# A third set of expert weight buffers and a six-expert TensorE loop in a mixture-of-experts decoder layer

## The reference

```python
def hier_moe(h, rg_w, rg_b, re_w, re_b, w_gate, w_up, w_down):
    ...                         # top-1 of 4 groups, top-2 of the 8 experts inside it
    for e in range(N_EXPERTS):  # 32
        y = (jax.nn.silu(t @ w_gate[e]) * (t @ w_up[e])) @ w_down[e]
        out = out + combine[:, e:e + 1] * y
```

## Time and profile before

| | us |
|---|---|
| three runs | 1025.98, 1027.39, 1028.46 |
| span of the profiled execution (first to last instruction) | 1026.5 |
| TensorE busy (matmuls) | 866.4 |
| first expert begins on TensorE | 460.98 |
| last matmul of expert 31 ends | 996.0 |

### The profile page before, as it was taken

The page is one execution under the profiler, slowest core; times in us unless marked ns, Lnnn a source line. Parts: engine busy times, 40 slices in busy tenths (PEclk is TensorE's granted clock), DMA queues, the critical chain, the costliest instruction groups (busy, mean ns, idle before and its releaser), DMA issues.

```text
span 1026.5 us, 15037 instructions
## 1 busy us (share of the span) xinstructions
PE 866.4 (84%) x5337; PEld 581.7 (57%) x5338; DVE 324.9 (32%) x576; ACT 194.9 (19%) x286; POOL 224.5 (22%) x270
## 2 busy tenths in 40 slices
PE   4999799999999999939899788788888888787760
PEld 4788487878877888825455344444454444444430
DVE  3894997560533445451011101001100110101016
ACT  5533216232432232400000000000000000000002
POOL 3566952422000000231111020111101111111100
PEclk9999799999999999959999999899998998999995
DMA  8693121623245752117999997579989999999956
GB/s 257 165 141 103 42 79 30 124 83 102 83 137 207 312 181 86 71 34 300 405 419 389 389 395 295 223 278 394 404 336 398 391 404 405 405 412 407 414 221 246
DMA packets 76278, 260.92 MB, mean 254 GB/s; under 512 B 29211, under 2 KB 30235, under 8 KB 67506
## 3 DMA queue, kind: packets, MB, share of 16 engines
q1 hardware_dynamic: 69842, 249.90, 65.9%
q0 software_dynamic: 6256, 10.51, 3.0%
q10 hardware_dynamic: 144, 0.02, 0.0%
HBM read 255.02 MB, written 14.42 MB: 262 GB/s over the span
## 4 chain that ended last, share of the span: by engine, by line
PE 58%; DMA 30%; DVE 5%; issue 3%; ACT 2%; POOL 0%; DVEq 0%; POOLq 0%; SPq 0%; ACTq 0%
PE ps L919 30%; DMA au<-in_exp_w_up 14%; PE ps L425 14%; DMA ssm<-in_exp_w_up 8%; PE ps L438 6%; DMA ssm<-in_exp_w_gate 2%; DMA pair<-h_scratch,idx_now 2%; PE ps L417 2%; PE ps L904 2%; DMA choice_rows<-pair,put_now 1%; PE ps L896 1%; DVE cv L1282 1%; PE ps L960 1%; PE ps L963 1%; DVE cv L639 1%
## 5 line engine op out<-in xcount | busy, mean ns | idle before, releaser
L425 PE MATMUL ps<-ssm,pair 128*64 128x256 f32 x1696 | 202.3, 395 | 38.1 <-DMA ssm<-in_exp_w_gate 17.7
L425 PEld LDWEIGHTS ps<-ssm,pair 128*64 128x64 f32 x1696 | 126.3, 142 | 123.8 <-issue 57.5
L587 DVE TENSOR_TENSOR pair<-pair,ps 128x256 f32<-128x256 f32 x32 | 13.5, 421 | 419.5 <-PE ps L425 419.5
L919 PE MATMUL ps<-h_hi,w_hi 128*128 128x512 f32 x288 | 113.4, 394 | 3.2 <-ACT ssm L1101 1.7
L919 PE MATMUL ps<-h_lo,w_hi 128*128 128x512 f32 x288 | 112.3, 390 | 0.0
L919 PE MATMUL ps<-h_hi,w_lo 128*128 128x512 f32 x288 | 112.3, 390 | 0.0
L1690 POOL TENSOR_TENSOR w_lo<-raw,w_hi 128x1024 fp32r<-128x1024 f32 x34 | 89.6, 2636 | 102.3 <-ACT w_hi L1108 101.9
L1108 ACT CAST w_hi<-raw 128x1024 fp32r<-128x1024 f32 x60 | 62.8, 1049 | 220.0 <-PE ps L919 219.2
L438 PE MATMUL ps<-ssm,pair 128*64 128x512 f32 x288 | 73.4, 656 | 18.3 <-DVE pair L594 8.8
L719 POOL COPY put_now<-put_u 128x1 uint32 (+1 forms) x35 | 6.4, 183 | 349.3 <-ACT late L653 305.3
L653 ACT COPY late<-ps 128x512 f32<-128x512 f32 x32 | 18.8, 586 | 325.0 <-PE ps L438 325.0
(11 more groups left out here) (281 smaller groups left out, 1053.8 us busy)
## 6 DMA issues: line engine op xcount, KB each, us to landing
ssm<-in_exp_w_gate SPq DMA_DIRECT2D x32, 2048.0 KB, 24.6
au<-in_exp_w_up SPq DMA_DIRECT2D x16, 2048.0 KB, 27.2
ssm<-in_exp_w_up SPq DMA_DIRECT2D x16, 2048.0 KB, 25.8
ssm<-in_exp_w_down SPq DMA_DIRECT2D x16, 2048.0 KB, 24.2
hl<-in_exp_w_down SPq DMA_DIRECT2D x16, 2048.0 KB, 26.7
raw<-in_w_in SPq DMA_DIRECT2D x40, 512.0 KB, 4.0
raw<-in_w_branch SPq DMA_DIRECT2D x12, 512.0 KB, 3.7
raw<-in_w_out SPq DMA_DIRECT2D x8, 512.0 KB, 8.4
```

Of the source, the lines that this page charges most:

```text
L425: t = nc.tensor.matmul(ps[CAP * h:CAP * (h + 1), bank, 0:HALF], xgT[b][:, k], w[:, k, HALF * h:HALF * (h + 1)], start=k == 0, stop=k == KD ...
L587: nc.vector.tensor_tensor(act_[b], silu[b], ps[:, B_UP, 0:HALF], ALU.mult).then_inc(act_ready, 1)
L919: t = nc.tensor.matmul(bank, lhs, rhs, start=k == 0 and n == 0, stop=k == 2 * count - 1 and n == 2)
```

## The change

There are now nine weight buffers, in three sets. The third set takes `hh` (gate), `mb` (up) and the first four pieces of `raw` (down). Expert e uses set e mod 3. The final norm's gain moves from `hh` to the fifth piece of `raw`. The other per-side buffers (tokens, activations, results) stay two deep.

The weights of expert 2 are loaded ahead of the stage: gate and up as soon as the last "o" product is done, down once the routing tables have been read (`idx_ready`). SyncE's loop reloads three experts per turn, each for the expert three places on. TensorE's loop has to know both the side (mod 2) and the set (mod 3) when it is built, so its body is now six experts, and it runs five times.

```diff
-        slots = [ssm[:, 4096 * s:4096 * (s + 1)] for s in range(4)] + [au[:], hl[:]]
+        slots = [ssm[:, 4096 * s:4096 * (s + 1)] for s in range(4)] + [
+            au[:], hl[:], hh[:], mb[:], raw[:, 0:4].rearrange("p a b -> p (a b)")]
...
-        EW = ({"gate": 0, "up": 1, "down": 2}, {"gate": 3, "up": 4, "down": 5})
+        EW = [{kind: SETS * s + n for n, kind in enumerate(KINDS)} for s in range(SETS)]
...
         def experts_sync(sp):
+            full(sp, ("o", 1, NT - 1))
+            weights(sp, 2, "gate", 2, ew_in[2]["gate"])
+            weights(sp, 2, "up", 2, ew_in[2]["up"])
             for s in range(2):
                 sp.wait_ge(h2_stored[s], 16 * 2)
-            full(sp, ("o", 1, NT - 1))
-            sp.dma_start(hh[:, 0:D], norm_final_g...).then_inc(gfin_in, 16)
+            sp.wait_ge(idx_ready, 1)
+            weights(sp, 2, "down", 2, ew_in[2]["down"])
+            sp.dma_start(gfin, norm_final_g...).then_inc(gfin_in, 16)
             sp.wait_ge(ov_ready, 1)
...
-            with sp.Fori(1, TURNS) as i:
-                for b in range(2):
-                    second_through(b, i * 2 + (b - 2))
-                    for kind in KINDS:
-                        sp.wait_ge(done[kind], i * 2 + (b - 1))
-                        weights(sp, b, kind, i * 2 + b, ew_in[b][kind])
+            def reload(e, w):
+                second_through(e - SETS)
+                for kind in KINDS:
+                    sp.wait_ge(done[kind], e - SETS + 1)
+                    weights(sp, w, kind, e, ew_in[w][kind])
+            with sp.Fori(1, NE // SETS) as i:
+                for w in range(SETS):
+                    reload(i * SETS + w, w)
+            for e in range(NE // SETS * SETS, NE):
+                reload(e, e % SETS)
...
-            with pe.Fori(1, TURNS) as i:
-                for b in range(2):
-                    turn(i * 2 + b, b, i, i + b, False)
+            with pe.Fori(1, (NE - 2) // (2 * SETS) + 1) as i:
+                for j in range(2 * SETS):
+                    turn(i * (2 * SETS) + (j - 4), j % 2, (j + 2) % SETS, i * 2 + (j - 4) // SETS,
+                         i * SETS + (j + 1) // 2 - 2, False)
```

More of the change, by code:

```diff
@@ L269, in trunk @@
         eps = stat[:, 60:61]
+        gfin = raw[:, 4]
         tables = raw[:, 1:4].rearrange("p a b -> p (a b)")
@@ L332, in trunk @@
         idx_ready, ov_ready, idx_copied, ov_idx_copied = (sem(n) for n in ("idx_ready", "ov_ready", "idx_copied", "ov_idx_copied"))
-        KINDS = ("gate", "up", "down")
+        KINDS, SETS = ("gate", "up", "down"), 3
         def per_side(name):
             return [sem(f"{name}{b}") for b in range(2)]
-        ew_in = [{k: sem(f"{k}_weights_in{w}") for k in KINDS} for w in range(2)]
+        ew_in = [{k: sem(f"{k}_weights_in{w}") for k in KINDS} for w in range(SETS)]
         done = {k: sem(f"{k}_done") for k in KINDS}
@@ L398, in trunk, with weights @@
         HALF = F // 2
-        def weights(eng, b, kind, e, signal):
+        def weights(eng, w, kind, e, signal):
             src = w_src[kind][e] if isinstance(e, int) else w_src[kind][bass.ds(e, 1)]
-            dst = slots[EW[b][kind]]
+            dst = slots[EW[w][kind]]
             if kind == "down":
-                dst = slot_h[EW[b][kind]]
+                dst = slot_h[EW[w][kind]]
                 if not isinstance(e, int):
@@ L418, in turn_x, with hidden @@
             return t
-        def hidden(b, kind, bank):
-            w = slot_k[EW[b][kind]]
+        def hidden(b, w_, kind, bank):
+            w = slot_k[EW[w_][kind]]
             for k in range(KD):
@@ L432, in turn_act, with down @@
             return t
-        def down(b, bank):
-            w = slot_h[EW[b]["down"]]
+        def down(b, w_, bank):
+            w = slot_h[EW[w_]["down"]]
             for n, (h, j) in enumerate((h, j) for h in range(2) for j in range(2)):
@@ L460, in experts_sync, with second_through @@
         def experts_sync(sp):
+            full(sp, ("o", 1, NT - 1))
+            weights(sp, 2, "gate", 2, ew_in[2]["gate"])
+            weights(sp, 2, "up", 2, ew_in[2]["up"])
             for s in range(2):
                 sp.wait_ge(h2_stored[s], 16 * 2)
[L463 to L464 removed]
+            sp.wait_ge(idx_ready, 1)
+            weights(sp, 2, "down", 2, ew_in[2]["down"])
+            sp.dma_start(gfin, norm_final_g.rearrange("(a d) -> a d", a=1).to_broadcast((P, D))).then_inc(gfin_in, 16)
             sp.wait_ge(ov_ready, 1)
[L467 removed]
+            def second_through(e):
                 flag, before = second_of(sp, e)
@@ L516, in experts_tensor, with turn @@
             pe.wait_ge(ov_ready, 1)
-            def turn(e, b, nth, next_xg, first):
+            def turn(e, b, w, nth, next_xg, first):
                 for kind, bank in (("gate", B_GATE), ("up", B_UP)):
-                    pe.wait_ge(ew_in[b][kind], nth * 16 + 16)
+                    pe.wait_ge(ew_in[w][kind], nth * 16 + 16)
                     if kind == "gate":
                         pe.wait_ge(xgT_ready, e + 1)
-                    hidden(b, kind, bank).then_inc(done[kind], 1)
+                    hidden(b, w, kind, bank).then_inc(done[kind], 1)
                 pe.wait_ge(xg_in[1 - b], next_xg * 16 + 16)
@@ L531, in turn @@
                 pe.wait_ge(actT_ready, e + 1)
-                pe.wait_ge(ew_in[b]["down"], nth * 16 + 16)
+                pe.wait_ge(ew_in[w]["down"], nth * 16 + 16)
                 if not first:
                     pe.wait_ge(res_ready, e - 1)
-                down(b, B_RES[b]).then_inc(done["down"], 1)
+                down(b, w, B_RES[b]).then_inc(done["down"], 1)
                 flag, before = second_of(pe, e)
@@ L541, in turn @@
                     pe.wait_ge(xgT2_ready, before + 1)
-                    hidden(b, "gate", B_GATE).then_inc(done2["gate"], 1)
-                    hidden(b, "up", B_UP).then_inc(done2["up"], 1)
+                    hidden(b, w, "gate", B_GATE).then_inc(done2["gate"], 1)
+                    hidden(b, w, "up", B_UP).then_inc(done2["up"], 1)
                     pe.wait_ge(act2_ready, before + 1)
@@ L546, in turn @@
                     pe.wait_ge(actT2_ready, before + 1)
-                    down(b, B_RES2).then_inc(done2["down"], 1)
+                    down(b, w, B_RES2).then_inc(done2["down"], 1)
                     pe.wait_ge(res2_ready, before + 1)
@@ L552, in experts_tensor @@
             for e in range(2):
-                turn(e, e, 0, e, True)
-            with pe.Fori(1, TURNS) as i:
-                for b in range(2):
-                    turn(i * 2 + b, b, i, i + b, False)
+                turn(e, e, e, 0, e, True)
+            with pe.Fori(1, (NE - 2) // (2 * SETS) + 1) as i:
+                for j in range(2 * SETS):
+                    turn(i * (2 * SETS) + (j - 4), j % 2, (j + 2) % SETS, i * 2 + (j - 4) // SETS,
+                         i * SETS + (j + 1) // 2 - 2, False)
             def over(o_, first):
@@ L566, in over @@
                     pe.wait_ge(res_ready, NE - 1)
-                hidden(0, "gate", B_GATE).then_inc(ov_done["gate"], 1)
-                hidden(0, "up", B_UP).then_inc(ov_done["up"], 1)
+                hidden(0, 0, "gate", B_GATE).then_inc(ov_done["gate"], 1)
+                hidden(0, 0, "up", B_UP).then_inc(ov_done["up"], 1)
                 pe.wait_ge(ov_act_ready, o_ + 1)
@@ L573, in over @@
                     pe.wait_ge(ov_res_ready, o_)
-                down(0, B_RES[0]).then_inc(ov_done["down"], 1)
+                down(0, 0, B_RES[0]).then_inc(ov_done["down"], 1)
             each_over(pe, over)
@@ L632, in final_norm @@
                 v.wait_ge(fin_step, i + 1)
-                nc.vector.scalar_tensor_tensor(x3[:, i], x3[:, i], stat[:, 24 + i:25 + i], hh[:, 0:D],
+                nc.vector.scalar_tensor_tensor(x3[:, i], x3[:, i], stat[:, 24 + i:25 + i], gfin,
                                                ALU.mult, ALU.mult).then_inc(outrow_ready, 1)
@@ L698, in picked_rows @@
             at = 2 * D * (i % 2)
-            return (mb if i < 2 else slots[EW[1]["gate"]])[:, at:at + 2 * D]
+            return slots[EW[2]["up" if i < 2 else "gate"]][:, at:at + 2 * D]
         def experts_gpsimd(gp):
```

2 lines of the change are left out of this document (1 added, 1 removed).

## The result

| | runs | median, us | lowest to highest |
|---|---|---|---|
| before, same chip | 10 | 1028.09 | 1025.98 to 1030.03 |
| changed | 10 | 1040.02 | 1033.55 to 1053.37 |
| changed, run again later | 4 | 1040.51 | 1035.70 to 1041.83 |
| before, beside the second row of runs | 9 | 1029.37 | |

The changed kernel is slower: ratio 1.0106, 95% interval 1.0084 to 1.0129, and 1.0098 (1.0065 to 1.0131) the second time. The forecast was 1020.5 us. The time lies in the range of 996 to 1060, on the other side of no change.

What follows compares the result with a forecast made beforehand. TensorE bounds first, then second blocks stop loads, then loads do. TensorE's 926.3 + 7 (start) + 9 x 6.2 (stalls) = 989.1 us, 6.9 before 996.0; span 1019.6 plus 0.9 gives 1020.5 us, range 996 to 1060.

Steps and rivals of the forecast that it cites:

- What bounds before, and what deeper buffers can address: Expert stage: TensorE alone would end at 926.3 us, not 996.0; deeper buffers can address the 69.7 us, less one item.
- Rival A: TensorE's loop code stays on the engine, only expert 3 stalls: faster, 1002.5 us; chance 0.25.
- 302 us that I gave the loads: Time from the issue of expert 14's loads, after expert 11, to the stage's end when loads set the pace.
- Code is refetched: TensorE's six-expert loop body does not fit, so code comes again each turn: nine stalls, 60 or more q8 packets.
- The price of a stall: Each TensorE wait for code, at jumps over second blocks and at loop returns, costs 6.2 us.
- The early loads against the start of the stage: Expert 2's early loads delay token stores by 3 us and expert 0's gather by 4: 7 us.
- TensorE is the later one by a little: At the stage's end TensorE finishes at 989.1 us, the loads at 983.5, so TensorE sets the end.
- it fits in whole: Under expert 16's second block the load allowed by the third set fits entirely.
- the count from which TensorE's sum passes before's: Number of TensorE stalls at which its own sum passes 996.0 us: 10.1, so slower from 11 stalls in all.
- the sign against it that I gave: The forecast would be wrong if q8 is silent after the first passage, or "issue" waits number 11 or more.
- Rival B: Three or more stalls per turn at TensorE's jumps over second blocks: slower, 1051.5 us at three; chance 0.27.
- Rival C: Code packets on the DMA engines hold up the weights, up to 40 us on one engine: 1027 to 1035; chance 0.08.
- Rival D: The third weight set isn't full when expert 2 begins; given no weight of its own.

Runs made afterwards that it cites:

- three-sided kernel with early loads: The three-sided kernel with expert 2's loads moved back to the changed kernel's early places: 1012.29 us, ratio 0.9839.
- three-sided kernel: Changed kernel with expert 2's loads late, token, result and bank buffers three deep, one activation buffer, TensorE loop body of three experts: 1001.0 us.
- the loop of four: Kernel before, two weight sets, with TensorE's loop body made four experts and the last two experts written out: 1029.89 us, ratio 0.9998.
- the copies: The loop of four plus two or four never-entered copies of a block's products at the body's end: 1078.39 us and 1085.96 us.
- late fill: Changed kernel with expert 2's gate and up loaded after the token stores, down after expert 0's gather: 1024.46 us, ratio 0.9942.
- three-sided pair: The three-sided kernel with late loads, 1001.0 us, against the three-sided kernel with early loads, 1012.29 us.

## Why the prediction was wrong

**What bounds before, and what deeper buffers can address: right.** Without the long loop and with late loads the third set takes 28 us off. Rival A, the case of kept code, stood at 1002.5 us with loads at their early places; the three-sided kernel with early loads is its nearest relative, and at 1012.29 it is 9.8 us later. Most of this is the start: its first expert begins at 473.52 us for 468, and the loads go on behind expert 11 at 675.4 for 669.1, 6.3 us later. From there the 302 us that I gave the loads were right, 978.4 - 675.4 = 303.0. The part behind the last matmul is 32.2 us for 30.5, and the median stands 0.8 more above the span. In the same profile the DMA share is 0.51 from 645 to 676 us, 15.2 us of idle time under expert 11's second block, as forecast (15 to 20). The issue of expert 14's gate and the last down product of that kernel, then the same issue in the changed one and its stretch under expert 16's second block:

```profile
675.39 0.34 SPq L412 DMA_DIRECT2D hh<-in_exp_w_gate  x1
974.77 3.65 PE L440 MATMUL ps<-hl,pair 128*64 128x512 f32 x16 [0.74 <-DVE pair L609]
...
694.25 0.34 SPq L412 DMA_DIRECT2D hh<-in_exp_w_gate  x1
776.00:788.00 12.00, 9.96 (x74) 5.36 (x70) 0.84 (x2) 0.58 (x1) 1.19 (x2) 1.00 0.52 192
```

**Code is refetched: right, also in its places.** The nine waits of over 2.5 us in the slowest execution stand at experts 3, 9, 15, 21, 27 and 8, 14, 20, 26, and q8 brings 74 packets for "60 or more".

**The price of a stall: off in both directions.** I read one price, 6.2 us, from one jump. From down to down a clean expert takes 12.70 us here. In the profile near the median the four returns take 8.2, 8.6, 9.5 and 9.2 us more, the jumps at 3 and 9 6.1 and 6.8, and those at 15, 21 and 27 nothing. Six small stalls that I had not listed (experts 5, 7, 13, 23, 25, 29) take 9.8 us together. Each price has two parts: behind expert 20's wait of 6.28 us the granted clock is 0.50 (1.2 GHz) from 832 to 836 us and 1.00 from 838 on, and the 32 gate products take 6.57 us for 3.62. Sum: 35.5 + 12.9 + 9.8 = 58.2, for 55.8. Here errors cancelled, and the sum wasn't far off; in the slowest execution the three jumps come on top, which fits the kernel's spread.

**The step that failed first: "The early loads against the start of the stage".** I took 3 + 4 = 7 us, with the stores bounded by "they cannot be held longer than the loads last". The bound was for the wrong thing. Before, only the fourth write of `late` waited, for a store that was nearly through (0.63 us). Under 4 MB of loads already the first store takes 12 us, and the third write waits for it:

```profile
441.08 0.75 DVE L1570 TENSOR_SCALAR late<-cv,stat 128x1024 f32<-128x1024 f32 x1 [8.11 <-DMA h_scratch<-late]
```

The loads were issued at 425.90 and 426.29 us, ahead of it. That they last to about 438 was right; 425.90 to 438 is 12 us, and the whole of it, less what the store took alone and what VectorE did meanwhile, fell on the path. Measured 8.1 for 3, the gather 3.2 for 4.

**The step that failed with it: "TensorE is the later one by a little" (989.1 against 983.5).** Both limits moved up, and the loads passed TensorE. TensorE waits for the weights of experts 30 and 31 at the very end, 2.8 and 3.8 us, so its own limit came to some 1002 (1008.8 less these two, an estimate); near expert 18 another 2.7 us is lost behind a second block's gather. The loads' limit came to 1008.8, 25.3 us above the forecast. Half of that had gathered when the loads went on behind expert 11 (694.25 us for 681.5: the start, this execution's first part, and stalls of 24.8 us for 18.6). The other half came behind it: 1008.8 - 694.25 = 314.5 us for 302. Of these 12.5 us, 5.8 are idle DMA time under expert 16's second block, of which I wrote that it fits in whole; in the three-sided kernel with early loads it does (share 1.01 from 700 to 765 us). The other 6.7 are not traced to one cause.

The end of the last matmul, forecast 989.1, came at 1008.8 us, 19.7 later:

| term | us |
|---|---|
| start of the stage, 12.3 for 7 | +5.3 |
| this execution's first part | +2.8 |
| second blocks, 56.7 for 54.5 | +2.2 |
| stalls, 58.2 for 55.8 | +2.4 |
| weights and gather (experts 30, 31, 18, 19) | +9.3 |
| clean experts, 12.70 for 12.75 and the ends | -2.5 |
| sum, of 19.7 | 19.5 |

The forecast stood 6.9 us below before's end, and five terms of one sign took that away and more. The two large ones are the start's 5.3 us, which I had sized too small, and the 9.3 us of waits, for which TensorE's sum has no term. The start's alone would have left the sign as it was; the waits' alone would have turned it, by 2.4 us. I had named the count from which TensorE's sum passes before's, 10.1 stalls; with the start at its true price it is (996.0 - 926.3 - 12.3) / 6.2 = 9.3, almost the nine that I forecast myself. With "issue" waits numbering 12 and 14, the sign against it that I gave has come too.

**Rival B** got the direction, not the mechanism: no turn has three large stalls. **Rival C** has little behind it: written out, the kernel fetches 39 packets in the same stretch and stands within 0.2 us of the three-sided kernel, which fetches two. **Rival D**: the third set was in time, expert 2 starts without a wait.

**How much code stays.** The Trainium skill (Runtime: NRT & Kernel Launch, Instruction fetch mechanics) gives eight packets of room; six stay and nine don't, as it says. That 7.4 don't either fits it only if more than the body passes through in a turn. The counts point that way. Without the code that comes once (30 packets with the loop of four, 1.4 and 2.8 more with the copies) each return brings (74 - 30) / 4 = 11 packets for the body of 9, (86 - 31.4) / 6 = 9.1 for that of 7.4 and (92 - 32.8) / 6 = 9.9 for that of 8.8, one to two more than the body holds. What these are, no run shows. The same section of the Trainium skill says that a taken branch to a target outside a window of two pages forces a fetch, by which the loop of four would stall at its returns. It goes back over six packets without a stall, so the measurement decides against that again.

**What stays open.** The late fill gains 16 us on the changed kernel where the three-sided pair gives 11.3 for the same move. One profile of each shows 2.2 us more of "issue" waits and 3.3 more of waits for weights with early loads; why they come together is not shown. Nor is it why the jumps at 15, 21 and 27 stall in some executions only.

## What to carry to other kernels

Before making an engine's loop longer, count its code in the packets that the first passage brings and compare with bodies known to stay (six packets here); if buffers of period 3 and 2 force a body of six, make both periods three, or drop the loop, since code that runs straight on costs nearly nothing here and only the return to code that is gone does. A transfer moved into "idle" DMA time is not free when small transfers on the critical path share that time: price it by how long the large one lasts, not by what the small one takes, and put it behind them. When a forecast rests on a margin of a few microseconds between two limits, price each small term from both ends before calling a direction.

## What the runs showed of the hardware

- A loop body of 6.0 packets of 16 KB stays on TensorE (3 packets fetched from 545 to 990 us); one of 9 does not (45 to 48 packets), nor does one of about 7.4 with a jump over 1.4 of them (52 packets).
- A return to code that is gone costs 8.2 to 9.5 us against a clean expert, 6.0 to 6.4 of them waiting and the rest in products at the lower granted clock; a return together with a jump over code that is never entered shows "issue" waits of 11.6 to 12.9 us. Code fetched straight on, 39 packets from 545 to 990 us, leaves 4.7 us of waits ahead of gate and up products in the whole stage.
- A 512 KB store takes 4.5 to 5.2 us, and 12.0 to 12.5 beside 4 MB of loads issued just ahead of it; a gather of 64 rows takes 2.7 to 2.8 us, and 6.0 to 6.6 behind one load of 2 MB.
